# The slots of the split weights are laid at unequal steps, 32 to 128 bytes further apart, in a one-core transformer kernel

## The reference, cut to what matters

```python
h = h + jnp.concatenate([o_g, o_m], axis=-1) @ w_out
m = rms_norm(h, mlp_norm)
h = h + jnp.square(jax.nn.relu(m @ w_mlp_up)) @ w_mlp_down
gate = jax.nn.sigmoid(rms_norm(h, ple_norm) @ w_ple_gate + b_ple_gate)
h = h + (p @ w_ple_proj) * gate
...
for i in range(2):                                   # the second kind
    h = rmsnorm(x, mix_norm[i])
    x = x + (pool_mixer(h) if i == 0 else chunk_attention(h))
    h = rmsnorm(x, ffn_norm[i])
    a = causal_dwconv3(h @ w_gate[i]) + conv_b[i]
    x = x + (silu(a) * (h @ w_val[i])) @ w_out[i]
```

## Time and profile before

| | |
|---|---|
| median of 3 runs | 1647.22 us (1647.04 to 1647.34) |
| profiled execution: span from first to last instruction | 1644.3 us, 2.9 us under the median |
| instructions | 19097 |
| TensorE matmul | 1638.7 us busy (100%), 8084 instructions |
| TensorE weight load | 1336.2 us (81%), beside the matmuls |
| VectorE / ScalarE / GpSimd | 939.2 us (57%) / 615.9 us (37%) / 84.6 us (5%) |
| HBM read | 149.98 MB, 94 GB/s over the span |

### The profile page before, as it was taken

The page is one execution under the profiler, slowest core; times in us unless marked ns, Lnnn a source line. Parts: engine busy times, 40 slices in busy tenths (PEclk is TensorE's granted clock), DMA queues, the critical chain, the costliest instruction groups (busy, mean ns, idle before and its releaser), DMA issues.

```text
span 1644.3 us, 19097 instructions
## 1 busy us (share of the span) xinstructions
PE 1638.7 (100%) x8084; PEld 1336.2 (81%) x8084; DVE 939.2 (57%) x1385; ACT 615.9 (37%) x828; POOL 84.6 (5%) x80
## 2 busy tenths in 40 slices
PE   9999999999999999999999999999999999999999
PEld 7877878888888888888888888877777888888887
DVE  6797665444333547577466457555655576366353
ACT  5576344322332346433222223355565333122121
POOL 1300000000000000000000000311201100000000
PEclk9999999999999999999999999999999999999999
DMA  5310227454454421223322223323221223222311
GB/s 187 116 36 27 103 93 128 120 89 130 87 111 85 135 88 52 77 103 107 124 83 96 103 83 100 123 78 101 77 76 52 77 103 104 102 102 94 110 59 71
DMA packets 28054, 155.94 MB, mean 95 GB/s; under 512 B 3712, under 2 KB 5392, under 8 KB 12096
## 3 DMA queue, kind: packets, MB, share of 16 engines
q1 hardware_dynamic: 26352, 149.75, 25.6%
q0 software_dynamic: 1328, 4.86, 5.0%
q10 hardware_dynamic: 288, 0.10, 0.0%
HBM read 149.98 MB, written 4.72 MB: 94 GB/s over the span
## 4 chain that ended last, share of the span: by engine, by line
PE 98%; ACT 1%; DVE 1%; POOL 0%; DMA 0%; issue 0%; SPq 0%; DVEq 0%
PE bank L585 26%; PE bank L587 26%; PE bank L586 26%; PE bank L591 3%; PE bank L593 3%; PE bank L592 3%; PE bank L1216 1%; PE bank L840 1%; PE bank L1226 1%; PE bank L1242 1%; PE bank L825 1%; PE bank L865 1%; PE bank L850 1%; PE bank L769 0%; PE bank L1102 0%; PE bank L1204 0%
## 5 line engine op out<-in xcount | busy, mean ns | idle before, releaser
L585 PE MATMUL bank<-AH,WH 128*128 128x512 f32 (+1 forms) x1150 | 451.4, 393 | 0.2 <-DVE X L1707 0.2
L587 PE MATMUL bank<-AH,WL 128*128 128x512 f32 (+1 forms) x1150 | 447.8, 389 | 0.0
L586 PE MATMUL bank<-AL,WH 128*128 128x512 f32 (+1 forms) x1150 | 447.6, 389 | 0.0
L1677 DVE TENSOR_TENSOR WL<-RAW,WH 128x2048 fp32r<-128x2048 f32 (+1 forms) x133 | 298.5, 2247 | 190.7 <-ACT WH L1287 190.7
L1287 ACT ACTIVATE WH<-RAW 128x2048 fp32r<-128x2048 f32 (+1 forms) x133 | 248.3, 1871 | 260.1 <-PE bank L587 240.3
L585 PEld LDWEIGHTS bank<-AH,WH 128*128 128x128 f32 (+1 forms) x1150 | 215.5, 187 | 48.0 <-issue 2.6
L587 PEld LDWEIGHTS bank<-AH,WL 128*128 128x128 f32 (+1 forms) x1150 | 215.5, 187 | 45.8
L586 PEld LDWEIGHTS bank<-AL,WH 128*128 128x128 f32 (+1 forms) x1150 | 215.6, 187 | 45.6 <-issue 1.0
L585 PE MATMUL bank<-HH,WH 128*128 128x512 f32 x608 | 239.6, 394 | 0.0
L587 PE MATMUL bank<-HH,WL 128*128 128x512 f32 x608 | 238.4, 392 | 0.0
L586 PE MATMUL bank<-HL,WH 128*128 128x512 f32 x608 | 236.0, 388 | 0.0
(11 more groups left out here) (306 smaller groups left out, 1732.9 us busy)
## 6 DMA issues: line engine op xcount, KB each, us to landing
RAW<-in_W SPq DMA_DIRECT2D x124, 1024.0 KB, 4.8
RAW<-in_W SPq DMA_DIRECT2D x9, 768.0 KB, 4.1
X<-in_XT SPq DMA_DIRECT2D x16, 256.0 KB, 5.5
ev_scratch<-ev POOLq DMA_DIRECT2D x16, 160.0 KB, 7.5
Gb<-ev_scratch SPq DMA_DIRECT2D x16, 128.0 KB, 2.9
Gb<-ev_scratch SPq DMA_DIRECT2D x16, 112.0 KB, 2.7
out<-X SPq DMA_DIRECT2D x7, 256.0 KB, 2.0
RAW<-in_W SPq DMA_DIRECT2D x2, 512.0 KB, 5.4
```

Source lines behind the costliest of these rows:

```text
L585: e.matmul(o, a, h, start=first, stop=False)
L586: e.matmul(o, a, l, start=False, stop=False)
L587: return e.matmul(o, c, h, start=False, stop=last)
L1677: e.tensor_tensor(k.WL[j][:, 0:n], k.RAW[RAW_OF[u]][:, 0:n], k.WH[j][:, 0:n].bitcast(F), SUB).then_inc(*WLO.mark(u))
```

## The change

Between the six weight slots gaps are laid: WH0 stays where it was, WH1 begins 32 bytes and WH2 64 bytes beyond its former place, WL0 128, WL1 192 and WL2 320 bytes. Everything that is allocated after them, from rb on, begins 352 bytes (the sum of the six gaps) later. The four tiles that lie over slots move with the slot. Nothing before the slots moves, and no instruction is added or taken away.

```diff
+WGAP = (32, 32, 64, 64, 128, 32)
...
     wh_at = a.at
-    k.WH = [a.tile(f"WH{i}", [P, UE], R) for i in range(NW)]
-    wl_at = a.at
-    k.WL = [a.tile(f"WL{i}", [P, UE], R) for i in range(NW)]
+    slot_at = [UE * 4 + gap for gap in WGAP]
+    k.WH = [a.over(f"WH{i}", [P, UE], wh_at + sum(slot_at[:i]), R) for i in range(NW)]
+    wl_at = wh_at + sum(slot_at[:NW])
+    k.WL = [a.over(f"WL{i}", [P, UE], wl_at + sum(slot_at[NW:NW + i]), R) for i in range(NW)]
+    a.at = wh_at + sum(slot_at)
...
-    k.qt = a.over("qt_", [P, 2, S], wl_at + slot * UE * 4)
-    k.kt = [a.over("kt0_", [P, 2, S], wl_at + slot * UE * 4 + 2 * S * 4), a.over("kt1_", [P, 2, S], gsil_at + 2 * S * 4)]
-    k.kd = a.over("kd", [P, 4, 256], wh_at + slot * UE * 4)
-    k.dd = a.over("dd", [P, 2, S], wh_at + slot * UE * 4 + 4 * 256 * 4)
+    k.qt = a.over("qt_", [P, 2, S], wl_at + sum(slot_at[NW:NW + slot]))
+    k.kt = [a.over("kt0_", [P, 2, S], wl_at + sum(slot_at[NW:NW + slot]) + 2 * S * 4), a.over("kt1_", [P, 2, S], gsil_at + 2 * S * 4)]
+    k.kd = a.over("kd", [P, 4, 256], wh_at + sum(slot_at[:slot]))
+    k.dd = a.over("dd", [P, 2, S], wh_at + sum(slot_at[:slot]) + 4 * 256 * 4)
```

## The result

The changed kernel takes 1676.26 us (median of 4, 1674.71 to 1676.40) against 1647.13 us before (4 runs, 1647.02 to 1647.34). The ratio is 1.0175, 95% interval 1.0161 to 1.0189: slower by 29 us. The direction was forecast, the size was not: I had said +9.1 us, and 1676.3 lies above my range, which ended at 1672.

A forecast was written before the change was run, and what follows sets the result against it. The prediction took TensorE's matmul pace as the bound; 9.1 (slots) + 0 (everything behind) + 0 (scratch and overlays) = +9.1 us on 1647.2 gave 1656.3 us, with a range of 1624 to 1672 us.

The forecast's parts named there:

- What bounds the kernel: Whole kernel: TensorE busy 100% at full clock, so time is a number of matmuls times a pace; no other engine matters.
- (a): Weight slots spread: 4101 matmuls lose equal offsets and go from 226.7 to 228.9 ns, +9.1 us (bounds -55 to +26).
- The ten steps at 232 after a change of tile: First ten steps going from HH to AH, 232 ns each before 226.7 returns; cited for the pace settling by how both sides meet.
- (b): Everything behind the slots 352 bytes later: HH and OH, 2016 matmuls, unequal before and after, 0 us (bounds -31 to +8.3).
- (c): Overlays in the slots and DVE and ACT scratch move too: 0 us, since those engines wait for TensorE.
- Worse than the forecast: All matmul stages: none settles, all run at the pH pace, +34 us, 1681 us; chance 0.07.
- The faster rival: AH and HH stages: unequal offsets free weight load and stream of each other, 1620 to 1643 us, middle 1634; chance 0.40.
- The rival of no change: All matmuls: pace comes from the moving stream alone, the weights' place has no say, 1647 us; chance 0.11.

The follow-up runs named there:

- experiment 2: Kernel before with only the six weight slots spread as in the change and everything behind them 512 bytes later: 1670.74 us against 1645.85, ratio 1.0146.
- experiment 3: Kernel before with slots unmoved and everything behind them 704 bytes later, so HH and OH have equal offsets: 1641.87 us against 1645.85, ratio 0.9973.
- experiment 1: Kernel before with slots unmoved and everything behind them 352 bytes later: 1657.45 us against 1645.85, ratio 1.0066.
- experiment 11: Kernel before with slots unmoved and everything behind them 192 bytes later: 1641.74 us against 1646.94, ratio 0.9968.
- experiment 14: Kernel before with WL, AL, HL 64 bytes off WH, AH, HH (equal modulo 256) and mixed products replaced in the triple: 1667.85 us against 1646.98, ratio 1.0129.

## Why the prediction was right in its direction and wrong in its size

**What bounds the kernel**: right. The pace of the 6117 matmuls accounts for 29.5 of the 30.2 us, at full clock and with the other engines' work as before.

**(a) the slots**: the direction was right, and so was the reason: with 512 columns the equal pair is the best of those seen, and the change takes it away. The step that failed is the choice of the value. I wrote "I take the value of the nearest row, the HH pace, since HH against WH is the one unequal relation that lasts for whole stages", 228.9 ns, and put the term at +9.1 us. In the changed kernel these 4101 matmuls cost 19.2 + 1.9 = 21.1 us, at 232.6 and 231.1 ns, under my upper bound of +26 from the 233.0 of pH. (The slots alone cost 24.9 us in experiment 2; that includes what they do to HH and OH there.) Of the six unequal offsets that were measured, in all slots or in HH (32, 64, 96, 128, 192, 224), one has 228.9 ns and five have 232.4 to 234.2. HH in the kernel before stood by chance at the one mild offset, 192. I had one witness for the usual case in my rows, pH at 233.0, which stood at offset 128, and passed it over because its stage is short. The ten steps at 232 after a change of tile are none: they are AH matmuls at offset 0 just behind HH at 192, and in experiment 3, where both are at 0, the same ten take 226.7 ns. That they agreed with pH was luck.

**(b) everything behind the slots**: I took 0 with the bounds -31 and +8.3 us. In the changed kernel HH and OH cost 7.7 + 0.7 = 8.4 us, at 233.2 and 232.8 ns. Part (b) costs 11.6 us alone (experiment 1), above the upper bound, since 96 modulo 256 gives 234.2 ns and pH had only 233.0. The step that failed is "Their relation to the weights was unequal and stays so", which treated unequal as one class.

**(c) the scratch and the overlays**: 0, right.

**The rivals.** "Worse than the forecast", at 1681 us, came within 5 us, though I gave it 0.07. Its reason was half right. The stages do settle, each slot for itself, but at 231 to 233 ns, none as good as before. The faster rival (the spread frees the two reads of each other) is refuted by the table: no unequal offset was below 226.7 ns. The rival of no change rested on the 256-column matmuls, which had exactly half of 226.7 ns at an unequal offset. That reading didn't carry: with the equal offset the same matmuls take 119.7 ns (experiment 11), so the offset has a say there too, only another one, and nothing follows from the half. The Trainium skill gives TensorE two independent read ports and says that it never waits ("SBUF — State Buffer", section "Who interferes with whom"); read as "addresses have no say", that would have given no change here. Against that reading stand 226.7 and 233.3 ns for a 64-byte shift of the standing tiles. Whether the two reads wait for each other, or something else does, no run here shows.

**The range** ended at 1672, because the case in which both stages run at 233 was kept out as unlikely. With the pH pace as the middle value for both (a) and (b) the same sum gives 26 + 8 = +34 us, where +29 came.

## What to carry to other kernels

When a kernel is a chain of back-to-back 512-column float32r matmuls, read the pace from the starts in each kind of stage. If two stages with the same instruction differ by 2 to 7 ns for each matmul, compare the places of the moving and the standing tiles modulo 256 bytes and lay every tile that meets another at an offset of 0: here one gap of 192 bytes was worth 0.3%, and the wrong gaps cost 2%. Don't carry the 0 over to matmuls of 256 columns without reading their pace too; here it was their slowest. When two rows give two values for an unknown case, the longer one isn't the likelier: a long stage shows how steady a pace is, and not how usual. HH and pH were one offset each, so the price of pH deserved as much weight as that of HH.

## What the runs showed of the hardware that I had not expected

The pace of a 128x512 float32r matmul depends on the offset between moving and standing tile, and it came back after 256 bytes: 226.7 ns at 0 and 256, 228.9 at 192, 232.4 or 233.3 at 128, 233.3 at 32, 64 and 224, 234.2 at 96. It isn't only a matmul's own pair that counts: in experiment 14 that pair was equal throughout, and the pace was 231.1. With 256 columns and the weights moving it is 119.7 to 120.0 ns at 0, and 113.3 or 117.8 at 64. The other engines and DMA have no part in it (the windows above).

The settled paces lie on a ladder. In three matmuls it is 680.0 ns (226.67), 686.7 (228.89), 693.3 (231.11) or 700.0 (233.33), in steps of 6.67 ns, which is 16 periods of the granted 2.4 GHz. The HH stage of experiment 1 repeats after seven steps, 231, 234, 235, 233, 232, 237 and 238 ns between its starts, and that fits as well: 1640 ns, 246 times 6.67. So does the AH stretch at offset 128, with 1626.7 ns for seven steps, 244 times 6.67. This looks like starts that fall into a fixed rhythm of that period and repeat once a whole number of them has passed. It would also explain why an odd load costs two thirds of the whole loss and not one third; that it is so wasn't shown, and what the rhythm belongs to isn't known.
